# A decoder layer on one core: the first phase reads x before its norm, and the scale is put on later

## The reference, cut to what matters

```python
h = rmsnorm(x, g_pre_mix)                 # x * rsqrt(mean(x*x) + EPS) * g
proj = h @ w_in
q_in, ckv, k_rope, lru_x, lru_y, gate_mla, gate_lru = split(proj)
kv = (rmsnorm(ckv, g_ckv) @ w_ukv)        # k_nope and v of 16 heads
sc = einsum(q, concat(k_nope, rope(k_rope))) * SOFTMAX_SCALE    # masked, softmax, times v
o_mla = o @ w_o_mla
hr = rg_lru(causal_dwconv(lru_x))
o_lru = (hr * gelu(lru_y)) @ w_o_lru
merged = sigmoid(gate_mla) * o_mla + sigmoid(gate_lru) * o_lru
x = x + rmsnorm(merged @ w_out, g_post_mix)
# then memory cross-attention and the ConvFFN, which the change does not touch
```

## Time and profile before

| what | value |
|---|---|
| median of 3 runs | 1754.73 us (1754.68 to 1756.06) |
| the profiled execution's own time | 1754.69 us |
| its span, first to last instruction | 1752.9 us |
| PE busy | 1735.5 us, 99% of the span |
| DVE, ACT, POOL busy | 1125.0 us, 910.3 us, 158.4 us |
| mean granted clock of TensorE | 0.997 |

### The profile page before, as it was taken

The page is one execution under the profiler, slowest core; times in us unless marked ns, Lnnn a source line. Parts: engine busy times, 40 slices in busy tenths (PEclk is TensorE's granted clock), DMA queues, the critical chain, the costliest instruction groups (busy, mean ns, idle before and its releaser), DMA issues.

```text
span 1752.9 us, 25415 instructions
## 1 busy us (share of the span) xinstructions
PE 1735.5 (99%) x9045; PEld 1481.1 (84%) x9045; DVE 1125.0 (64%) x1382; ACT 910.3 (52%) x1165; POOL 158.4 (9%) x183
## 2 busy tenths in 40 slices
PE   8999999999999999999999999999999999999997
PEld 7888888888888888888888888888888888888886
DVE  6666665454788874446557687776367776467765
ACT  6656664343577763334456575554345555245552
POOL 0002220000244430000000000000000000000000
PEclk9999999999999999999999999999999999999999
DMA  7645457555455565555655446555455556545552
GB/s 239 209 128 157 147 174 257 204 192 192 150 180 179 182 238 192 192 192 193 238 170 180 157 145 192 191 189 218 168 179 182 181 180 240 188 145 190 191 217 95
DMA packets 214366, 325.77 MB, mean 186 GB/s; under 512 B 5888, under 2 KB 162212, under 8 KB 207268
## 3 DMA queue, kind: packets, MB, share of 16 engines
q1 hardware_dynamic: 208532, 315.53, 53.7%
q10 hardware_dynamic: 5776, 9.44, 1.5%
HBM read 322.85 MB, written 2.10 MB: 185 GB/s over the span
## 4 chain that ended last, share of the span: by engine, by line
PE 98%; DMA 1%; DVE 0%; ACT 0%; SPq 0%; issue 0%; DVEq 0%
PE ps L486 50%; PE ps L534 40%; PE ps L502 3%; PE ps L593 1%; PE ps L746 1%; PE ps L568 1%; PE ps L680 1%; PE ps L709 0%; PE ps L685 0%; DMA big_a<-in_x 0%; DMA raw<-in_w_in 0%; PE ps L702 0%; PE ps L710 0%; PE ps L832 0%; PE ps L848 0%; DVE raw L1992 0%
## 5 line engine op out<-in xcount | busy, mean ns | idle before, releaser
L1426 DVE TENSOR_TENSOR wsp<-raw,wsp 128x2048 fp32r<-128x2048 f32 (+2 forms) x308 | 678.8, 2224 | 342.4 <-ACT wsp L1011 339.1
L1011 ACT ACTIVATE wsp<-raw 128x2048 fp32r<-128x2048 f32 (+2 forms) x308 | 562.3, 1847 | 311.7 <-PE ps L534 299.5
L486 PE MATMUL ps<-asp,wsp 128*128 128x512 f32 (+1 forms) x3072 | 543.4, 339 | 0.7 <-DVE asp L1840 0.7
L486 PEld LDWEIGHTS ps<-asp,wsp 128*128 128x128 f32 x3072 | 471.0, 188 | 70.9 <-issue 0.9
L534 PE MATMUL ps<-wsp,hsp 128*128 128x512 f32 x2304 | 526.2, 390 | 0.0
L534 PEld LDWEIGHTS ps<-wsp,hsp 128*128 128x128 f32 x2304 | 432.1, 188 | 89.3
L486 PE MATMUL ps<-hsp,wsp 128*128 128x256 f32 (+1 forms) x1952 | 353.7, 340 | 1.6 <-DVE hsp L1480 1.6
L486 PEld LDWEIGHTS ps<-hsp,wsp 128*128 128x128 f32 x1952 | 300.0, 188 | 45.5 <-issue 2.2
L1022 ACT ACTIVATE cr<-ps 128x256 f32<-128x256 f32 x189 | 70.9, 381 | 207.1 <-PE ps L486 180.8
L534 PE MATMUL ps<-wsp,asp 128*128 128x512 f32 x768 | 175.3, 389 | 0.0
L534 PEld LDWEIGHTS ps<-wsp,asp 128*128 128x128 f32 x768 | 144.0, 188 | 29.8
(11 more groups left out here) (208 smaller groups left out, 895.8 us busy)
## 6 DMA issues: line engine op xcount, KB each, us to landing
raw<-in_w_up SPq DMA_DIRECT2D x88, 1024.0 KB, 5.4
raw<-in_w_in SPq DMA_DIRECT2D x64, 1024.0 KB, 5.4
raw<-in_w_down SPq DMA_DIRECT2D x44, 1024.0 KB, 5.0
raw<-in_w_in SPq DMA_DIRECT2D x32, 768.0 KB, 4.4
raw<-in_w_o_mla SPq DMA_DIRECT2D x16, 1024.0 KB, 5.2
raw<-in_w_o_lru SPq DMA_DIRECT2D x16, 1024.0 KB, 5.2
raw<-in_w_out SPq DMA_DIRECT2D x16, 1024.0 KB, 4.9
raw<-in_w_ukv SPq DMA_DIRECT2D x8, 1024.0 KB, 5.3
```

The costliest lines, as they stand in the source:

```text
L486: mm = pe.matmul(ps[:, bank, 0:w], lhs(part, k), x[:, 0:w], start=(f and part == 0), stop=(l and n == 1))
L1011: act.activation(wsp[:, p0 % SLOTS, 0, 0:n], raw[:, p0 % SLOTS, 0:n], ACT.Copy).then_inc(hi_done, 1)
L1426: dve.tensor_tensor(wsp[:, slot, 1, 0:n], raw[:, slot, 0:n], wsp[:, slot, 0, 0:n].bitcast(F32), ALU.subtract).then_inc(lo_done, 1)
```

## The change

**The start.** x isn't multiplied by r any more. ACT's queue carries g_pre_mix and then its half of x; SP's queue carries x quarters and the first four weight pieces by turns, and then the small rows. PE turns each quarter of x as it lands; ACT's squares (now one instruction per 128 tokens) and r are made inside the loop over PH_A's pieces. The first piece is split in two halves (`first_hi`, `first_lo`), and PE takes its products k by k instead of tile by tile. There are 6 and 4 warm matmuls where there were 11 and 12. POOL clears a smaller tile first.

**Where r goes.** Two diagonal matrices `x_diag` and a product with ones give `X_ROW`, r of each token along the free axis, in all partitions. DVE multiplies KRAW by it; the ckv norm gets r twice (`nst` 18 and 14); the scores are scaled in two instructions by SCALE * r of the queries, one for each block of 128 queries, in place of one instruction; the sigmoid of gate_mla takes r as its scale.

**In PH_OM** `hsp` is scaled in place, in eight pairs of k tiles, at the pieces that `H_PAIRS` lists: trip 0 at pieces 6 and 7, trip 1 at 0, 1, 2, 4, 5 and 6. For each pair DVE adds the two parts into `HT` and multiplies by X_ROW (three instructions), ACT writes the new high part (`h_hi`), DVE the new low part (`h_low`, at the next pair; the last one in piece 7 of trip 1, behind that piece's `lo`). PH_LRU waits for all eight (`h_lo`).

```diff
+H_PAIRS = [(0, 6), (0, 7), (1, 0), (1, 1), (1, 2), (1, 4), (1, 5), (1, 6)]
...
-        def load_x(eng, m):
...
-            for b in range(4):
-                eng.dma_start(a_tok[:, m, quarter(b)], x_tok[:, m, quarter(b)]).then_inc(x_in[4 * m + b], 16)
+        def load_x(eng, m, b):
...
+            eng.dma_start(a_tok[:, m, quarter(b)], x_tok[:, m, quarter(b)]).then_inc(x_in[4 * m + b], 16)
...
-            eng.wait_ge(prow_zero, 1)
+            eng.wait_ge(prow_zero, 2)
...
-            load_x(sp, 0)
-            sp.wait_ge(prow_zero, 1)
-            sp.dma_start(GROW[0:KT, :], a["g_pre_mix"][0].rearrange("(r c) -> r c", c=P)).then_inc(g_in0, 16)
...
-            sp.wait_ge(x_in[2], 16)
+            load_x(sp, 0, 0)
...
+            load_x(sp, 0, 1)
...
+            load_x(sp, 0, 2)
+            load_x(sp, 0, 3)
+            first_cols(2)
+            first_cols(3)
...
-            for c in range(2, 8):
+            for c in range(4, 8):
...
-            warm(11)
+            warm(6)
...
-                        pe.wait_ge(x_scaled, k // 2 + 2)
+                        for m in range(2):
+                            pe.wait_ge(x_in[4 * m + k // 4], 16)
...
-            warm(12)
...
+            warm(4)
...
-                arrive(PH_A, 0, c)
...
-                pe.wait_ge(x_lo, 2 * c + 2)
...
+                    if c == 0 and k == 0:
+                        pe.wait_ge(first_lo, 1)
+                    else:
+                        arrive(PH_A, 0, c)
+                    pe.wait_ge(x_lo, 2 * c + k + 1)
+                    first, last = (c, k) == (0, 0), (c, k) == (7, 1)
...
-                                 2 * c + k, 1, hsp, c == 0 and k == 0, c == 7 and k == 1, False)
-                for m in range(2):
-                    for k in range(2):
+                                 2 * c + k, 1, hsp, first, last, False)
+                    for m in range(2):
...
-                                           wv[part][:, k, 0:RANK], start=(c == 0 and k == 0 and t == 0),
-                                           stop=(c == 7 and k == 1 and t == 2))
-                    if c == 7 and m == 0:
-                        mm.then_inc(ckv_mm, 1)
+                                           wv[part][:, k, 0:RANK], start=(first and t == 0), stop=(last and t == 2))
+                        if last and m == 0:
+                            mm.then_inc(ckv_mm, 1)
...
+                    pe.wait_ge(x_diag_made, 2)
+                    for m in range(2):
+                        pe.matmul(ps[:, 6, T + m * P:T + (m + 1) * P], ones[:, :], x_diag[m], start=True, stop=True)
...
+            pe.wait_ge(h_lo, KT // 2)
...
-            load_x(act, 1)
+            act.wait_ge(prow_zero, 1)
+            act.dma_start(GROW[0:KT, :], a["g_pre_mix"][0].rearrange("(r c) -> r c", c=P)).then_inc(g_in0, 16)
+            for b in range(4):
+                load_x(act, 1, b)
...
-            def gate(ph, i, j, bank, dst):
+            def gate(ph, i, j, bank, dst, scale=1.0):
...
-                act.activation(dst, ps[:, bank, :], ACT.Sigmoid).then_inc(tile_out, 1)
+                act.activation(dst, ps[:, bank, :], ACT.Sigmoid, scale=scale).then_inc(tile_out, 1)
...
-            for b in range(4):
-                for m in range(2):
-                    act.wait_ge(x_in[4 * m + b], 16)
-                    act.activation(b_tok[:, m, quarter(b)], a_tok[:, m, quarter(b)], ACT.Square,
-                                   accum_out=nst[:, 3, 4 * m + b:4 * m + b + 1]).then_inc(x_sq, 1)
-            root(1, nst[:, 3, 10:12], nst[:, 3, 8:10])
-            for p in range(LEAD):
-                hi(PH_A, 0, p)
...
+            def x_square(m):
...
+                for b in range(4):
+                    act.wait_ge(x_in[4 * m + b], 16)
+                act.activation(b_tok[:, m, :], a_tok[:, m, :], ACT.Square, accum_out=nst[:, 3, 8 + m:9 + m]).then_inc(x_sq, 1)
...
-            x_high(range(4))
+            x_high(range(2))
+            half = RANK + ROPE
+            act.wait_ge(landed[0], 16)
+            act.activation(wsp[:, 0, 0, 0:half], raw[:, 0, 0:half], ACT.Copy).then_inc(first_hi, 1)
+            act.activation(wsp[:, 0, 0, half:2 * half], raw[:, 0, half:2 * half], ACT.Copy).then_inc(hi_done, 1)
+            x_high(range(2, 4))
+            hi(PH_A, 0, 1)
...
+                if c in (1, 3):
+                    x_square(c // 2)
+                if c == 4:
+                    root(1, nst[:, 3, 10:12], nst[:, 3, 8:10])
...
-                    gate(PH_GM, i, 2 * half + m, [1, 2, 0, 3][2 * half + m], a_tok[:, m, quarter(2 * i + half)])
+                    gate(PH_GM, i, 2 * half + m, [1, 2, 0, 3][2 * half + m], a_tok[:, m, quarter(2 * i + half)],
+                         scale=nst[:, 3, 14 + m:15 + m])
...
+                    if (i, c) in H_PAIRS:
+                        n = H_PAIRS.index((i, c))
+                        act.wait_ge(h_scaled, n + 1)
+                        act.activation(hsp[:, 2 * n:2 * n + 2, 0:T], HT[n % 2], ACT.Copy).then_inc(h_hi, 1)
...
-            tok_rms(1, 3, slice(0, 2), x_sq, 8)
...
-            def x_scale(b):
...
-                for m in range(2):
-                    x = a_tok[:, m, quarter(b)]
-                    dve.tensor_scalar(x, x, nst[:, 3, 14 + m:15 + m], None, ALU.mult).then_inc(x_scaled, 1)
...
-            x_scale(0)
-            lo(PH_A, 0, 0)
...
-            x_scale(1)
+            half = RANK + ROPE
+            dve.wait_ge(first_hi, 1)
+            dve.tensor_tensor(wsp[:, 0, 1, 0:half], raw[:, 0, 0:half], wsp[:, 0, 0, 0:half].bitcast(F32),
+                              ALU.subtract).then_inc(first_lo, 1)
+            dve.wait_ge(hi_done, 1)
+            dve.tensor_tensor(wsp[:, 0, 1, half:2 * half], raw[:, 0, half:2 * half], wsp[:, 0, 0, half:2 * half].bitcast(F32),
+                              ALU.subtract).then_inc(lo_done, 1)
...
-            x_scale(2)
-            x_scale(3)
...
+                if c == 4:
+                    v, r = nst[:, 3, 8:10], nst[:, 3, 14:16]
+                    dve.wait_ge(x_sq, 2)
+                    dve.tensor_scalar(v, v, 1.0 / D, EPS, ALU.mult, ALU.add).then_inc(var_ready, 1)
+                    dve.wait_ge(root_ready, 1)
+                    newton(v, nst[:, 3, 10:12], nst[:, 3, 12:14], r)
+                    for m in range(2):
+                        dve.tensor_scalar(x_diag[m], ident[:, :], nst[:, 3, 14 + m:15 + m], None, ALU.mult).then_inc(x_diag_made, 1)
+                    own.mark(dve.tensor_scalar(nst[:, 3, 16:18], r, SCALE, None, ALU.mult))
+                    own.mark(dve.tensor_tensor(nst[:, 3, 18:20], r, r, ALU.mult))
+                if c == 7:
+                    dve.wait_ge(angle_ready, 2)
+                    dve.wait_ge(par_turned, 1)
+                    own.mark(dve.tensor_copy(X_ROW, ps[:, 6, T:2 * T]))
...
-                ins = dve.tensor_tensor(KRAW[to:to + 64, :], ps[64:P, 4, 0:T], cr[64:P, 3, :], ALU.add)
-            ins.then_inc(tile_out, 1)
+                own.mark(dve.tensor_tensor(KRAW[to:to + 64, :], ps[64:P, 4, 0:T], cr[64:P, 3, :], ALU.add))
+            own.wait()
...
+            own.link(dve.tensor_tensor(v, v, nst[:, 3, 18:20], ALU.mult))
...
-            dve.wait_ge(par_turned, 1)
+            dve.tensor_tensor(KRAW, KRAW, X_ROW, ALU.mult).then_inc(tile_out, 1)
...
-                dve.tensor_scalar(ckv_diag[m], ident[:, :], nst[:, 2, 14 + m:15 + m], None, ALU.mult).then_inc(ckv_scaled, 1)
+                dve.tensor_scalar(ckv_diag[m], ident[:, :], nst[:, 2, 14 + m:15 + m], nst[:, 3, 14 + m:15 + m], ALU.mult, ALU.mult).then_inc(ckv_scaled, 1)
...
-                attention(i, PH_Q, i, lambda part: part and q_out(PH_Q, i), 8)
+                attention(i, PH_Q, i, lambda part: part and q_out(PH_Q, i), 10)
...
-            assert own.n == n0 + 8
-            own.n, own.off = n0 + 8 * PH_Q.trips, 0
+            assert own.n == n0 + 10
+            own.n, own.off = n0 + 10 * PH_Q.trips, 0
...
+            def h_low(n):
...
+                dve.wait_ge(h_hi, n + 1)
+                dve.tensor_tensor(hsp[:, 2 * n:2 * n + 2, T:2 * T], HT[n % 2], hsp[:, 2 * n:2 * n + 2, 0:T].bitcast(F32),
+                                  ALU.subtract).then_inc(h_lo, 1)
...
+                    if (i, c) in H_PAIRS:
+                        n = H_PAIRS.index((i, c))
+                        if n:
+                            h_low(n - 1)
+                        hs = hsp[:, 2 * n:2 * n + 2, :].bitcast(F32)
+                        own.link(dve.tensor_tensor(HT[n % 2], hs[:, :, 0:T], hs[:, :, T:2 * T], ALU.add))
+                        own.mark(dve.tensor_tensor(HT[n % 2][:, 0, :], HT[n % 2][:, 0, :], X_ROW, ALU.mult))
+                        own.wait()
+                        dve.tensor_tensor(HT[n % 2][:, 1, :], HT[n % 2][:, 1, :], X_ROW, ALU.mult).then_inc(h_scaled, 1)
+                    if (i, c) == (1, 7):
+                        h_low(KT // 2 - 1)
...
-            pool.memset(scr[:, 0:7 * P], 0.0).then_inc(prow_zero, 1)
```

(20 more changed lines are left out.)

## The result

| | before | after |
|---|---|---|
| median | 1754.9 us (17 runs, 1754.57 to 1756.06) | 1759.14 us (17 runs, 1756.73 to 1759.67) |
| profiled execution, and its span | 1754.69, 1752.9 us | 1759.26, 1757.4 us |
| ratio | | 1.0019, 95% interval 1.0012 to 1.0027 |

The forecast was 1756.8 us in 1751.5 to 1760.5. The medians differ by 4.2 us, the ratio says 3.3 (0.0019 x 1755) with 2.1 to 4.7 in its interval: slower, at about the 0.2% that was called the limit. The runs after fall into two clusters, eight from 1756.7 to 1758.3 and nine from 1759.1 to 1759.7; the profiled one is of the upper.

What follows compares the result with a forecast made beforehand. PE, busy 99% of the span, was taken to bound the kernel. Against the profiled 1754.69 us: -7.1 (start) + 0.45 (products with ones) + 7.2 (wait) + 1.6 (clock) = +2.15, so 1756.8 us, range 1751.5 to 1760.5.

Steps and rivals of the forecast that it cites:

- What bounds: Whole kernel: PE, busy 99%, hardly stops after its first product at 16.61; only an earlier start or less PE work wins.
- Landing: piece 0 lands at 7.9, x's first pair near 5.6: Start of PH_A: two queues share some 400 GB/s; x is turned and split in time, PE starts at 9.5 us.
- the term -7.1 of the sum: Start of PH_A: first product at 9.5 instead of 16.6 us, a gain of 7.1 us.
- At the start itself ... 0: Start: PE stands for 1.5 us after warm matmuls and turning; clock cost 0, as an earlier 1.6 us wait left it at 1.00.
- PH_A runs on, ACT and DVE keep up: PH_A: pieces land and split in time, 0.9 us to spare at the tightest; ACT and DVE cause no delay, 0 us.
- Attention: 0: Attention rounds: two score instructions for one cost 0.16 us by the second head, hidden under 0.76 us of cover; 0.
- PH_OM: a new wait of 7.2: Before PH_LRU's first product: PE waits 7.2 us for the last h_low, as ACT/DVE bodies take 7.0 us against PE's 5.45.
- The clock: 1.6: Behind the wait at PH_LRU: the granted clock falls to half rate, costing 1.6 us more, bounds 0 and 3.2.
- B: Rival, PH_OM: bodies of at most about 5.5 us hide the scaling and keep the head start, 1748.1 us; chance 0.13.
- C: Rival, start: not fed, gain 4.1 instead of 6.65, and the wait at PH_LRU comes as well, 1759.4 us; chance 0.13.
- D: Rival, wait at PH_LRU: the clock doesn't fall there, the rest as forecast, 1755.2 us; chance 0.07.

## Why the prediction held, and where it was off

- **What bounds.** Right: all the differences are in PE's waits and its clock. Sizes of other engines' work (DVE 17 us busier) left no trace in the time.
- **"Landing: piece 0 lands at 7.9, x's first pair near 5.6"**, the term -7.1 of the sum, failed. The step took the two queues to share equally from the first byte on, and the piece to be the last to land. The piece landed at 6.5, earlier than forecast, and x's pair at 7.1, later; behind x came a chain of 3.66 us, in which the piece's split waits its turn on ACT and DVE behind x's parts. The first product was at 10.86 for 9.5, outside the bounds of 8.9 to 10.5. The unequal sharing is shown (0.50 against 0.04 MB), but not that it made x late: with 0.32 against 0.22, PE was let go at 6.92.
- **"At the start itself ... 0" for the clock** failed too. PE stood 2.39 us for x, turned it at half speed (1.94 us for 1.04), and the first half of piece 0 was slow (2.78 for 1.75). That is the other part of what is missing: PH_A ended at 43.28, forecast 41.4. With six more warm matmuls 0.5 us of it came back. The slow half piece belongs to this execution rather than to the change: three traces with the same start (pairs early, no scaling, PE busy in its wait) have 1.99 us for it, and PH_A's end at 42.2 to 42.4.
- **PH_A runs on, ACT and DVE keep up.** Right: no PE wait between 10.86 and PH_OM, and the products with ones took 0.44 us (forecast 0.45). DVE had 1.25 us of idle time left before k_rope, where 0 was expected, as PE came later.
- **Attention: 0.** Right. PE turns every 21.16 us (123.49 to 144.65), before 21.15. The cover shrank more than worked out: POOL ends at 144.24 (143.27 + 0.97), PE turns at 144.65, 0.41 us of cover for 0.76, so the two instructions cost 0.35, not 0.16. The instructions themselves show it: the two take 0.74 us together where the one took 0.56, for each of two heads.
- **PH_OM: a new wait of 7.2.** Right in place, mechanism and nearly in size: bodies of 6.92 (7.0), wait 6.51 (7.2). That it is this wait, and its order, is shown by the kernels with h_low moved and with the pairs early.
- **The clock: 1.6.** Right in kind, shown by the kernel with warm matmuls in the wait; the size was 2.63, inside the bounds of 0 to 3.2, since the low stretch was 5.6 us long and not 3.1. The Trainium skill (TensorE: Matmul & The Clock Gate, Part 1) says that the moment of release varies from run to run; the traces agree, since with one and the same start the eight turning matmuls took 1.07 us in the trace of the kernel with h_low moved and 1.94 in that of the changed kernel.
- **Rivals.** B's outcome (hidden scaling, 1748.1) is what the kernel with the pairs early gives, at 1749.13, but not by B's condition: a body with a pair is 6.92 us long there too (404.61 to 411.53), and what hides it is the bodies without one between and behind. C's mechanism, a start that is fed late, was there in part: 1.9 us of the 2.5 that it took, some of that from slow products and not from feeding. D is refuted in this kernel.
- Errors of both signs met: gain short by 1.9, wait by 0.7 shorter, clock 1.0 longer, +2.2 in all; 1756.8 against 1759.14.

Open: the 0.17 us between PH_A and PH_OM; the late landing above; and the two clusters of runs. Of these the traces show only that the same start differs between executions: 2.78 us for the first half piece in the changed kernel's, 1.99 in three others, and in that of h_low moved a granted clock of 0.50 from 8.2 to 15.0. That this makes the clusters is likely but not shown.

## What to carry to other kernels

When PE is 99% busy, a head start is worth what no later wait takes back, so look for the first place where moved work has to be finished, and add up the ring of engines that makes it, not each engine's busy time: ACT and DVE were each idle for over 2 us in a turn of 6.9, and that turn was still longer than PE's 5.45. Work with a distant deadline belongs early and with free bodies between, and its last step shouldn't stand behind the splitting of a piece that nobody needs yet. A long wait of PE can be charged twice, once for itself and once for the clock behind it (6.5 and 2.6 us here), and matmuls that compute nothing recovered the second part. At a start, follow the chain that ended last before blaming a transfer: what PE waits for by name (the split) need not be what came late (x, or the gain).

## What was not expected of the hardware

- Behind a wait of 2.5 us between products the granted clock went to 0.50 (from about 438.3 to 441.7, so it fell a microsecond after PE had gone on), and behind one of 2.0 us at the start of the same trace as well (from 8.2 to 15.0), while one of 1.6 us in the trace before left it at 1.00. The low stretch behind 6.5 us lasted 5.6 us of PE work.
- The profile's granted clock reads 1.00 from the first microsecond in every trace, also where the matmuls take 421 ns and later ones of the same shape 275. Until its first fall, which in the kernel before comes at 9.4, it told nothing of the rate. At a start the durations have to be read, not the clock row.
- Two DMA queues on the same engines do not share equally at once: 0.50 against 0.04 MB from 3 to 5 us, with a 0.59 MB transfer issued 0.2 us before the other queue's 0.26 MB. With that order turned round it was 0.32 against 0.22, and yet the 0.26 MB let PE go no earlier (6.92).
